# A transformer layer on one core: normalisation passes moved between engines, tile loads on another queue, and the last product in another order

## The chip, the core and the metric

The kernel runs on one core of a Trainium2 chip, in one launch. TensorE (PE) multiplies matrices into PSUM, VectorE (DVE) and ScalarE (ACT) work elementwise, GpSimd (POOL) works elementwise on SBUF, and SyncE (SP) issues DMAs. ScalarE issues some DMAs too. The metric is the device time of the launch in microseconds. Lower is better.

## The reference, cut to what matters

One post-norm layer over 2048 tokens of 1024 features: a mixer of two attentions and a short convolution, then a squared-ReLU MLP. Each half ends in a gated residual and a layer norm with a gain and a bias. The change touches what follows the mixer:

```python
def layer_norm(x, g, b):
    mu = x.mean(-1, keepdims=True)
    var = jnp.square(x - mu).mean(-1, keepdims=True)
    return ((x - mu) * lax.rsqrt(var + EPS)) * g + b
...
y_x = jnp.concatenate([mo, go, co], axis=-1) @ w_o                 # output projection
x = layer_norm(ALPHA * x + mx[:, 2] * y_x, ln1_g[l], ln1_b[l])
y_x = jnp.square(jax.nn.relu((x * (1.0 + mx[:, 4]) + mx[:, 3]) @ w1)) @ w2
x = layer_norm(ALPHA * x + mx[:, 5] * y_x, ln2_g[l], ln2_b[l])
```

## The kernel before, in words

Matmuls run on numbers split in two parts: a high part (ScalarE copies and rounds it) and a low part (VectorE subtracts the high part from the number). A product of two split numbers is three matmuls: high x high, high x low, low x high. Six stages follow each other. A stage begins when the one before has ended on all engines. Only the last two are touched.

**stage_mix, the output projection** (line 1259 on, about 1764 to 2006 us). It works over 16 tiles of 128 tokens, in the order of TILE. For tile s, TensorE (`work`, then `turn`) multiplies the mixed tile `m_hi`, `m_lo` (1 MB, loaded by `load_m`, two buffers) by w_o, 48 matmuls of 128x512, and then transposes the normalised rows of the tile before. VectorE (`work`) applies the gate, adds the residual, takes the statistics, waits for ScalarE's square root, centres and scales (`o_r`) and multiplies by the gain `ln_g` into `x1`. GpSimd adds the bias `ln_b` (line 1488). SP stores x1. ScalarE makes the modulated, transposed tile (`stream`), and then, per pair of tiles, the high parts of the seven operands for the MLP (`highs`, line 1397). Five of these are sums of two blocks, which GpSimd forms (`sums`, line 1482, two buffers). VectorE makes the low parts (`lows`, line 1467). Results that don't fit in SBUF go through a ring of three buffers to DRAM on SP's queue. VectorE's order is: tile 2q, the low parts of the pair before, tile 2q+1. ScalarE issues `load_x` and `load_m` for tile s+2 behind the square root of tile s.

**stage_mlp, the MLP** (line 1520 on). Both matrices are multiplied by Strassen's scheme: seven products of half-size blocks in place of eight, over sums of blocks. The first matrix (2009 to 2632 us) isn't touched. For the second, the 2048 tokens are two halves `hf`; per half there are seven products in the order of ORDER2, 14 in all (PRODS). A product is 8 chunks of 24 matmuls (128x512) over four row blocks `tt`, into four PSUM banks. For each chunk SP loads x (512 KB) and one or two blocks of w2 (512 KB each); where there are two, GpSimd forms their sum (`chunk_sum`, line 2090); ScalarE makes two high parts (`chunk_high`), VectorE two low parts (`chunk_low`, lines 1936 and 1938). Products 2 and 5 need no sum. The function `steps` lays down one order for all engines: at chunk tau they prepare chunk tau + 5 (AHEAD), then treat the product that ended before. In its chunks 0 and 1 they add its four banks into the result quarters `yacc` (`evacuate` on VectorE, line 2016, `first` on ScalarE for a quarter's first use); in 2 and 3 they apply gate and residual and take the statistics of quarters that are complete (`before_ln`, lines 2024 to 2029; PRES names them, x1 is read again from DRAM into two buffers); in 4 and 5 they finish complete tiles (FINISH, after products 6 and 7): ScalarE centres and scales (line 1904), VectorE multiplies by the gain (line 2055), GpSimd adds the bias (line 2118), SP stores. SP's queue holds these stores between the chunk loads. GpSimd's bias passes stand between its chunk sums.

The last product runs apart: for each row block tt in turn all 8 chunks, 48 matmuls. `last` treats each row block as it comes: add, gate, residual, statistics, norm and, one row block later, the gain.

## Time and profile before

| | us |
|---|---|
| median of 3 runs | 3297.54 (3292.43 to 3299.11) |
| the profiled execution | 3291.43 |
| its span, first to last instruction | 3289.6 |
| TensorE busy | 3093.5 |
| VectorE busy | 2354.3 |
| GpSimd busy | 1470.7 |
| ScalarE busy | 1365.4 |

All times in the rows are microseconds from the start of the span of one profiled execution. The time of a launch is the span and some 2 us around it. A matmul's duration in the rows is longer than its step to the next one, as they are pipelined: starts are to be compared. An idle time in brackets is that of the engine before the instruction, with what ended it.

### The profile page before, as it was taken

What the parts mean: (1) busy time and instruction counts of PE and PEld (TensorE: products, weight loads), DVE (VectorE), ACT (ScalarE), POOL (GpSimd) and SP (SyncE); (2) the same over time, 40 slices, a digit from 0 to 9 for tenths busy, and PEclk for the clock granted to TensorE, in tenths of its full rate; (3) what the DMA queues carried; (4) which work ended last, traced back from release to release, by engine and by line L of the source; (5) the groups of instructions that cost most, each with busy time, mean ns of one, the idle gap of its engine ahead of it and who ended that gap; (6) DMA issues with size and microseconds to landing.
All of it is one profiled execution on the core that took longest, in us unless ns stands there. A gap on an engine that the chain in (4) does not pass through costs nothing. (4 is left out here: it accounts for less than half of the span.)

```text
span 3289.6 us, 38729 instructions
## 1 busy us (share of the span) xinstructions
PE 3093.5 (94%) x13713; PEld 2283.2 (69%) x13713; DVE 2354.3 (72%) x3209; ACT 1365.4 (42%) x1931; POOL 1470.7 (45%) x857
## 2 busy tenths in 40 slices
PE   6999958999999999999998897999999999999996
PEld 3888845565565655656565775888788888887885
DVE  4344447777777777777765888777778768887778
ACT  3222222434344343444442435655555554344432
POOL 1233301576665766765662445333333223444453
PEclk8999977999999999999998998999999999999998
DMA  6222378123332223230214577444734488777873
GB/s 236 62 88 85 90 239 271 53 57 83 87 82 74 56 61 87 67 80 14 54 35 165 224 260 292 161 158 156 291 144 150 152 311 293 289 265 275 299 288 137
DMA packets 235708, 515.51 MB, mean 157 GB/s; under 512 B 26704, under 2 KB 101840, under 8 KB 223312
## 3 DMA queue, kind: packets, MB, share of 16 engines
q1 hardware_dynamic: 224688, 472.39, 43.0%
q10 hardware_dynamic: 10848, 40.90, 3.5%
q8 instruction: 99, 1.62, 0.2%
q14 instruction: 73, 0.60, 0.1%
HBM read 356.64 MB, written 156.57 MB: 156 GB/s over the span
## 5 line engine op out<-in xcount | busy, mean ns | idle before, releaser
L1032 DVE TENSOR_REDUCE h_mpart<-a_mx 128x1 f32<-128x512 f32 x920 | 568.3, 636 | 260.6 <-PE a_mx L1121 251.7
L978 POOL TENSOR_TENSOR a_acc_p<-a_acc_p,a_pf 128x1024 f32<-128x1024 f32 x240 | 582.0, 2425 | 234.2 <-ACT a_pf L1014 213.0
L1014 ACT ACTIVATE a_pf<-a_sc 128x1024 f32<-128x1024 f32 x432 | 443.0, 1026 | 475.5 <-PE a_sc L1147 470.2
L2148 PE MATMUL f_bank<-slot_hi,f_wx 128*128 128x512 f32 x1280 | 401.0, 390 | 9.0 <-DVE f_wx L1931 7.0
L2081 POOL TENSOR_TENSOR f_work<-raw_rows 128x512 f32<-128x512 f32 x160 | 220.9, 1382 | 369.8 <-DVE f_wx L1931 366.4
L2090 POOL TENSOR_TENSOR f_y<-f_y,raw_rows 128x1024 f32<-128x1024 f32 x80 | 222.0, 2776 | 333.2 <-DMA raw_rows<-in_w 333.2
L2148 PE MATMUL f_bank<-slot_lo,f_wx 128*128 128x512 f32 x896 | 350.0, 391 | 0.0
L2148 PEld LDWEIGHTS f_bank<-slot_hi,f_wx 128*128 128x128 f32 x1280 | 240.9, 188 | 60.4 <-DVE f_wx L1931 7.4
L2156 PE MATMUL f_bank<-slot_hi 128*128 128x512 f32 x672 | 263.9, 393 | 12.4 <-DVE slot_lo L1938 12.4
L1952 DVE TENSOR_TENSOR f_work<-f_work,f_bank 128x512 f32<-128x512 f32 x256 | 174.4, 681 | 134.3 <-ACT f_work L1821 123.1
L2156 PE MATMUL f_bank<-slot_lo,slot_hi 128*128 128x512 f32 x672 | 263.6, 392 | 0.0
L2156 PE MATMUL f_bank<-slot_hi,slot_lo 128*128 128x512 f32 x672 | 263.4, 392 | 0.0
L500 PE MATMUL p_main<-win_hi,u_hi 128*128 128x512 f32 (+2 forms) x528 | 198.2, 375 | 20.3 <-POOL u_lo L443 19.6
L1938 DVE TENSOR_TENSOR slot_lo<-f_y,slot_hi 128x1024 fp32r<-128x1024 f32 x84 | 138.6, 1650 | 94.1 <-ACT slot_hi L1805 93.5
L1121 PE MATMUL a_mx<-a_mk_hi,a_mq_hi 96*128 96x512 f32 (+1 forms) x480 | 186.7, 389 | 10.7 <-DVE h_mpart L1032 10.5
L500 PE MATMUL p_main<-win_lo,u_hi 128*128 128x512 f32 (+2 forms) x528 | 196.3, 372 | 0.0
L500 PE MATMUL p_main<-win_hi,u_lo 128*128 128x512 f32 (+2 forms) x528 | 196.1, 371 | 0.0
L2148 PEld LDWEIGHTS f_bank<-slot_lo,f_wx 128*128 128x128 f32 x896 | 169.2, 189 | 34.9
L1164 PE MATMUL a_o<-a_pf,h_gv 128*64 128x512 f32 x864 | 192.8, 595 | 0.0
L1164 PE MATMUL a_o<-a_pf,a_v 128*64 128x512 f32 x864 | 192.7, 595 | 0.0
L1147 PE MATMUL a_sc<-a_mq_hi,a_mk_hi 97*128 97x512 f32 x432 | 177.2, 410 | 0.0
L1147 PE MATMUL a_sc<-h_gq_hl,h_gk_hh 128*128 128x512 f32 x432 | 176.3, 408 | 0.7 <-ACT h_gq_hm L994 0.7
(288 smaller groups left out, 6545.1 us busy)
## 6 DMA issues: line engine op xcount, KB each, us to landing
raw_rows<-s_hx SPq DMA_DIRECT2D x112, 512.0 KB, 4.1
f_y<-in_w SPq DMA_DIRECT2D x112, 512.0 KB, 5.2
raw_rows<-in_w SPq DMA_DIRECT2D x80, 512.0 KB, 5.8
raw_rows<-in_w SPq DMA_DIRECT2D x32, 1024.0 KB, 4.8
s_hx<-stream SPq DMA_DIRECT2D x128, 256.0 KB, 2.7
s_hx<-f_work SPq DMA_DIRECT2D x96, 256.0 KB, 2.0
a_wa<-in_w_ada SPq DMA_DIRECT2D x8, 2048.0 KB, 9.0
s_mix<-low SPq DMA_DIRECT2D x96, 128.0 KB, 2.5
```

Of the source, the lines that this page charges most:

```text
L500: mm = nc.tensor.matmul(main[:, b, 0:cn], lhs[s][:, k], rhs[:, k, c0:c0 + cn], start=(k == 0 and rhs is w_hi and lhs is u_hi), stop=(k == ...
L978: nc.gpsimd.tensor_tensor(acc[:, :], left[:, :], pf[(b * KT + kt) % NPF][:, :], ALU.add).then_inc(added_p, 1)
L1014: nc.scalar.activation(pf[n % NPF][:, :], sc[n % 2][:, :], ACT.Exp, scale=SCALES[0 if is_mla(b) else 1]).then_inc(exped, 1)
L1032: nc.vector.reduce_max(mpart[b % 2][:, s, k:k + 1], mx[c % 2][:, 0:CHUNKS[k][1]], AX.X).then_inc(mx_read, 1)
L1121: nc.tensor.matmul(mx[c % 2][:, 0:width], lhs, rhs, start=True, stop=True).then_inc(mx_done, 1)
L1147: mm = nc.tensor.matmul(out, x, y, start=(m == 0), stop=(m == len(ops) - 1))
L1164: mm = nc.tensor.matmul(o_ps[half * DH:(half + 1) * DH, :], v[0 if is_mla(b) else 1][:, kt], pf[n % NPF][:, half * QB:(half + 1) * QB], st ...
L1952: nc.vector.tensor_tensor(t, t, bank[:, (NP * n + pos) % 8, :], plus(sign)).then_inc(c_set, 1)
L2081: nc.gpsimd.tensor_tensor(out, w1_part(n, first), w1_part(n, second), plus(sign)).then_inc(sum_set, 1)
L2090: nc.gpsimd.tensor_tensor(y1[cc % YN], y1[cc % YN], y2[k % Y2N], plus(sign)).then_inc(y_sum, 1)
L2148: mm = nc.tensor.matmul(by_pair(bank[:, m % 8, :]), w[:, k], x[s][:, :, k * P:(k + 1) * P], start=(k == 0 and j == 0), stop=(k == 3 and j ...
L2156: mm = nc.tensor.matmul(bank[:, 4 * (pr % 2) + tt, :], x[s][:, f, tok], y[s][:, 2 + f, :], start=(start and j == 0), stop=(stop and j == 2))
```

## The change

In the output projection the loads of the mixed tiles move from ScalarE's queue to SP's. `load_m(s + 2)` goes ahead of the ring stores and of the store of x1, and the ring stores come one tile later in the program. The bias moves from GpSimd to VectorE.

In the MLP the order of products becomes 2, 4, 3, 1, 6, 5, 7. PRES, DVE_ADDS and ACT_FIRST follow from it. ScalarE no longer centres, GpSimd no longer adds the bias: VectorE does (y - mean) * gain and then y * rstd + bias. ScalarE's first writes of the second half wait for the stored tiles of their own quarter only. The last product takes its first three chunks over all row blocks together. Gate and residual of the last quarter are applied before it, and its banks are scaled by the gate on their own and added.

```diff
         @block.sync
         def _(sp):
+            def load_m(s):
+                t = TILE[s]
+                if s >= 2:
+                    sp.wait_ge(y_done, s - 1)
+                for part, m in enumerate((m_hi, m_lo)):
+                    sp.dma_start(raw(m[s % 2]), g.mix[part][t]).then_inc(mix_in[s % 2], 16)
+            load_m(0)
             sp.dma_start(ln_cols[:, :], a["ln1_cols"]).then_inc(cols_in, 16)
...
             for s, t in enumerate(TILE):
+                if s + 2 < TT:
+                    load_m(s + 2)
+                if s and s % 2 == 0:
+                    store_sums(s // 2 - 1)
                 sp.wait_ge(x1_set, s + 1)
                 sp.dma_start(g.x1[t * P:(t + 1) * P, :], x1[s % 2]).then_inc(x1_stored[s % 2], 16)
-                p = s // 2
-                if s % 2 and p < PAIRS:
-                    for pos in range(NP):
-                        use = ring_use(p, pos)
-                        if use is None:
-                            continue
-                        sp.wait_ge(lo_set, NP * p + pos + 1)
-                        for part, at in enumerate((ring_hi, ring_lo)):
-                            sp.dma_start(g.uc[p // 4, pos, part][:, p % 4, :], raw(at[use % RING])).then_inc(uc_stored[use % RING], 32 // 2)
             sp.wait_ge(cols_in, 16)
...
         @block.scalar
-            def load_m(s):
-                t = TILE[s]
-                if s >= 2:
-                    act.wait_ge(y_done, s - 1)
-                for part, m in enumerate((m_hi, m_lo)):
-                    act.dma_start(raw(m[s % 2]), g.mix[part][t]).then_inc(mix_in[s % 2], 16)
...
                 nc.scalar.activation(rstd[:, :], var[:, :], ACT.Sqrt).then_inc(std_set, 1)
                 if s + 2 < TT:
                     load_x(s + 2)
-                    load_m(s + 2)
                 if s and (s - 1) % 2:
                     highs((s - 1) // 2)
...
                     dve.wait_ge(x1_stored[s % 2], 16 * (s // 2))
                 nc.vector.tensor_tensor(x1[s % 2], at, ln_g, ALU.mult).then_inc(scaled, 1)
+                dve.wait_ge(scaled, s + 1)
+                nc.vector.tensor_tensor(x1[s % 2], x1[s % 2], ln_b, ALU.add).then_inc(x1_set, 1)
                 assert seen[0] == STEPS, seen
...
-                pool.wait_ge(scaled, s + 1)
-                nc.gpsimd.tensor_tensor(x1[s % 2], x1[s % 2], ln_b, ALU.add).then_inc(x1_set, 1)
...
-        ORDER2 = (5, 3, 2, 4, 1, 6, 7)
+        ORDER2 = (2, 4, 3, 1, 6, 5, 7)
...
-        DVE_ADDS = {5: (), 3: (("12", 1),), 2: (("22", -1),), 4: (("11", 1), ("21", 1)), 1: (("11", 1), ("22", 1)), 6: (("22", 1),), 7: (("11", 1),)}
-        ACT_FIRST = {5: (("12", 1), ("11", -1)), 3: (("22", 1),), 2: (("21", 1),), 4: (), 1: (), 6: (), 7: ()}
+        DVE_ADDS = {2: (), 4: (("21", 1),), 3: (("22", 1),), 1: (("11", 1), ("22", 1)), 6: (("22", 1),), 5: (("12", 1), ("11", -1)), 7: (("11", 1),)}
+        ACT_FIRST = {2: (("21", 1), ("22", -1)), 4: (("11", 1),), 3: (("12", 1),), 1: (), 6: (), 5: (), 7: ()}
...
-        PRES = {3: ("12",), 4: ("21",), 6: ("22",), 7: ("11",)}
-        PRE_ORDER = ("12", "21", "22", "11")
+        PRES = {4: ("21",), 6: ("22",), 5: ("12",), 7: ("11",)}
+        PRE_ORDER = ("21", "22", "12", "11")
         FINISH = {6: range(4, 8), 7: range(0, 4)}
-
-        def steps(prep, evacuate, before_ln, finish, last):
+        TOGETHER = 3
+
+        def steps(prep, evacuate, before_ln, finish, last, before_last=lambda tt: None):
...
                     for key in PRES.get(i, ()):
                         for tt in (2 * k - 4, 2 * k - 3):
                             before_ln(hf, key, tt, pr)
-                elif k < 6 and i in FINISH:
-                    finish(hf, FINISH[i], k - 4)
+                elif k < 6:
+                    if i in FINISH:
+                        finish(hf, FINISH[i], k - 4)
+                    if pr == LAST - 1:
+                        for tt in (2 * k - 8, 2 * k - 7):
+                            before_last(tt)
             last()
...
 
             def store_out(hf, t):
-                k = finish_index(hf, t)
-                if k == 15:
-                    sp.wait_ge(last_set, 1)
-                else:
-                    sp.wait_ge(biased, k + 1)
-                sp.dma_start(a["out"][0, hf * 1024 + t * P:hf * 1024 + (t + 1) * P, :], yacc[t]).then_inc(out_stored, 16)
+                sp.wait_ge(scaled, finish_index(hf, t) + 1)
+                sp.dma_start(a["out"][0, hf * 1024 + t * P:hf * 1024 + (t + 1) * P, :], yacc[t]).then_inc(last_stored if hf else out_stored[t // 4], 16)
 
             for n in range(PAIRS):
...
-                        act.wait_ge(out_stored, 16 * 8)
+                        act.wait_ge(out_stored[int(key[0]) - 1], 16 * 4)
                     elif pr == 0:
...
-                nc.scalar.activation(yacc[t], yacc[t], ACT.Identity, scale=rstd[:, t:t + 1], bias=shift[:, t:t + 1]).then_inc(centred, 1)
-
             def before_ln(hf, key, tt, pr):
                 if key in ("22", "11") and tt == 3:
...
-                link(nc.vector.tensor_tensor(shift[:, c], mv[:, c, 0], rstd[:, c], ALU.mult))
-                nc.vector.tensor_scalar(shift[:, c], shift[:, c], -1.0, None, ALU.mult).then_inc(norm_ready, 1)
 
             def scale(hf, t):
                 k = finish_index(hf, t)
+                dve.wait_ge(rows_in, 32)
+                nc.vector.scalar_tensor_tensor(out=yacc[t], in0=yacc[t], scalar=mv[:, t, 0:1], in1=ln_g, op0=ALU.subtract, op1=ALU.mult).then_inc(centred, 1)
                 dve.wait_ge(centred, k + 1)
-                dve.wait_ge(rows_in, 32)
-                nc.vector.tensor_tensor(yacc[t], yacc[t], ln_g, ALU.mult).then_inc(scaled, 1)
+                nc.vector.scalar_tensor_tensor(out=yacc[t], in0=yacc[t], scalar=rstd[:, t:t + 1], in1=ln_b, op0=ALU.mult, op1=ALU.add).then_inc(scaled, 1)
...
+            def residual(hf, key, tt):
+                k = pre_index(hf, key, tt)
+                half = int(key[1]) - 1
+                y = quad(key, tt)
+                dve.wait_ge(gate_step, 2)
+                nc.vector.tensor_tensor(y, y, gate[:, half * 512:(half + 1) * 512], ALU.mult).then_inc(mid, 1)
+                dve.wait_ge(mid, k + 1)
+                dve.wait_ge(x1_in[k % X1N], 16 * (k // X1N + 1))
+                nc.vector.scalar_tensor_tensor(out=y, in0=x1[k % X1N], scalar=ALPHA, in1=y, op0=ALU.mult, op1=ALU.add).then_inc(pre_set, 1)
+                dve.wait_ge(pre_set, k + 1)
+
+            def before_last(tt):
+                dve.wait_ge(add_set, adds_before(LAST))
+                residual(1, "11", tt)
+
             def last():
                 for tt in range(4):
-                    evacuate(LAST, tt)
-                    before_ln(1, "11", tt, LAST)
-                    norms(1, tt, 1, pre_index(1, "11", tt))
-                    if tt:
-                        scale(1, tt - 1)
-                scale(1, 3)
-                dve.wait_ge(scaled, TT)
-                nc.vector.tensor_tensor(yacc[3], yacc[3], ln_b, ALU.add).then_inc(last_set, 1)
-            steps(chunk_low, evacuate, before_ln, finish, last)
+                    k, part = pre_index(1, "11", tt), y1[tt % YN][:, 0, :]
+                    y = quad("11", tt)
+                    dve.wait_ge(tt_done, 4 * LAST + tt + 1)
+                    nc.vector.tensor_tensor(part, bank[:, 4 * (LAST % 2) + tt, :], gate[:, 0:512], ALU.mult).then_inc(last_mid, 1)
+                    dve.wait_ge(last_mid, tt + 1)
+                    nc.vector.tensor_tensor(y, y, part, ALU.add).then_inc(add_set, 1)
+                    dve.wait_ge(add_set, adds_before(LAST) + tt + 1)
+                    nc.vector.bn_stats(stats[:, tt, 0, :], y).then_inc(stat_set, 1)
+                    norms(1, tt, 1, k)
+                    scale(1, tt)
+            steps(chunk_low, evacuate, before_ln, finish, last, before_last)
...
-            def bias(hf, t):
-                k = finish_index(hf, t)
-                pool.wait_ge(scaled, k + 1)
-                pool.wait_ge(rows_in, 32)
-                nc.gpsimd.tensor_tensor(yacc[t], yacc[t], ln_b, ALU.add).then_inc(biased, 1)
...
+            for c in range(TOGETHER):
+                cc = LAST * CH + c
+                pe.wait_ge(clo, 2 * cc + 2)
+                for f in range(2):
+                    for tt in range(4):
+                        if c == 0 and f == 0:
+                            pe.wait_ge(add_set, adds_before(LAST - 2) + len(DVE_ADDS[PRODS[LAST - 2][1]]) * (tt + 1))
+                        two(LAST, tt, chunk_slot(cc), f, c == 0 and f == 0, False)
             for tt in range(4):
-                pe.wait_ge(add_set, adds_before(LAST - 2) + len(DVE_ADDS[PRODS[LAST - 2][1]]) * (tt + 1))
-                for c in range(CH):
+                for c in range(TOGETHER, CH):
                     cc = LAST * CH + c
                     pe.wait_ge(clo, 2 * cc + 2)
                     for f in range(2):
-                        mm = two(LAST, tt, chunk_slot(cc), f, c == 0 and f == 0, c == CH - 1 and f == 1)
+                        mm = two(LAST, tt, chunk_slot(cc), f, False, c == CH - 1 and f == 1)
                 mm.then_inc(tt_done, 1)
```

## Rows read from the trace of the kernel before

**Rows 1.** The page: busy us of each engine, share of the span, instructions

```profile
PE 3093.5 (94%) x13713; PEld 2283.2 (69%) x13713; DVE 2354.3 (72%) x3209; ACT 1365.4 (42%) x1931; POOL 1470.7 (45%) x857
```

**Rows 2.** Windows: length; busy of PE, PEld, DVE, ACT, POOL; clock; DMA share; GB/s

```profile
1796.00:2002.00 206.00, 177.03 (x801) 144.58 (x799) 169.18 (x259) 75.79 (x185) 87.50 (x51) 0.94 0.62 232
2633.00:3211.00 578.00, 569.81 (x2500) 470.87 (x2499) 451.81 (x383) 247.08 (x261) 238.88 (x85) 0.99 0.80 289
...
3211.00:3290.00 79.00, 49.19 (x195) 38.69 (x193) 64.22 (x101) 17.74 (x20) 29.51 (x11) 0.80 0.34 128
```

**Rows 3.** Waits, 1760 to 2010 us: who waited for whom, us in total, times, longest

```profile
DVE o_ring_lo L1467 <- ACT o_ring_hi L1397: 18.4, 20, 2.9
...
PE o_y L1502 <- DMA slot_lo<-s_mix: 16.7, 7, 3.3
...
PE o_t_x L1511 <- DVE o_r L1451: 14.6, 5, 9.6
```

**Rows 4.** Timeline, VectorE and GpSimd, output projection: start, duration, line, tiles, [idle before]

```profile
1809.18 1.23 DVE L1437 SCALAR_TENSOR_TENSOR o_r<-o_x,o_r 128x1024 f32<-128x1024 f32 x1
...
1816.75 0.69 DVE L1467 TENSOR_TENSOR slot_lo<-o_total,slot_hi 128x512 fp32r<-128x512 f32 x1
...
1824.16 2.52 DVE L1467 TENSOR_TENSOR o_ring_lo<-o_total,o_ring_hi 128x512 fp32r<-128x512 f32 x1 [0.28 <-ACT o_ring_hi L1397]
...
1835.32 2.34 DVE L1437 SCALAR_TENSOR_TENSOR o_r<-o_x,o_r 128x1024 f32<-128x1024 f32 x1
...
1915.88 1.23 DVE L1436 TENSOR_TENSOR o_r<-o_y,o_gate 128x1024 f32<-128x1024 f32 x1 [1.79 <-PE o_y L1502]
...
1823.29 2.85 POOL L1488 TENSOR_TENSOR o_x<-o_x,o_ln_b 128x1024 f32<-128x1024 f32 x1
...
2001.03 2.34 POOL L1488 TENSOR_TENSOR o_x<-o_x,o_ln_b 128x1024 f32<-128x1024 f32 x1 [8.09 <-DVE o_x L1456]
```

**Rows 5.** Timeline, TensorE and ScalarE (ACTq is its DMA issues), 1891 to 1894 us

```profile
1891.24 0.73 PE L1502 MATMUL o_y<-low,slot_hi 128*128 128x512 f32 x2 [3.16 <-DMA slot_lo<-s_mix]
...
1893.86 0.49 ACTq L1363 DMA_DIRECT2D slot_hi<-s_mix  x1
```

**Rows 6.** Timeline, TensorE, second MLP matrix and its last product

```profile
2633.24 0.48 PE L2156 MATMUL f_bank<-slot_hi 128*128 128x512 f32 x1
...
3008.11 0.80 PE L2156 MATMUL f_bank<-slot_hi 128*128 128x512 f32 x1 [6.16 <-DVE slot_lo L1938]
...
3211.29 0.39 PE L2156 MATMUL f_bank<-slot_hi 128*128 128x512 f32 x1
...
3217.86 0.39 PE L2156 MATMUL f_bank<-slot_hi,slot_lo 128*128 128x512 f32 x1
...
3231.36 0.80 PE L2156 MATMUL f_bank<-low 128*128 128x512 f32 x1 [0.54 <-DVE slot_lo L1938]
...
3267.99 0.39 PE L2156 MATMUL f_bank<-low,slot_lo 128*128 128x512 f32 x1
```

**Rows 7.** Timeline, GpSimd, 2980 to 3010 us

```profile
2983.19 6.65 POOL L2118 TENSOR_TENSOR f_work<-f_work,f_ln_b 128x1024 f32<-128x1024 f32 x2 [10.97 <-DVE f_work L2055]
```

**Rows 8.** Timeline, VectorE, the last row blocks

```profile
3270.37 0.69 DVE L2029 BATCH_NORM_STATS2 cond_pad<-f_work 128x6 f32<-128x512 f32 x1
...
3272.54 0.16 DVE L2047 TENSOR_TENSOR cond_pad<-cond_pad 128x1 f32<-128x1 f32 x1
...
3274.15 0.68 DVE L2016 TENSOR_TENSOR f_work<-f_work,f_bank 128x512 f32<-128x512 f32 x1
...
3285.37 1.23 DVE L2070 TENSOR_TENSOR f_work<-f_work,f_ln_b 128x1024 f32<-128x1024 f32 x1
```

**Rows 9.** Timeline, VectorE, four residual quarters; and its costliest group, 2633 to 3290 us

```profile
3231.23 0.68 DVE L2024 TENSOR_TENSOR f_work<-f_work,f_gate 128x512 f32<-128x512 f32 x1
...
3238.81 0.69 DVE L2029 BATCH_NORM_STATS2 cond_pad<-stream 128x6 f32<-128x512 f32 x1
...
L1936 DVE TENSOR_TENSOR slot_lo<-raw_rows,slot_hi 128x1024 fp32r<-128x1024 f32 x83 | 145.9, 1758 | 19.3 <-ACT slot_hi L1799 18.8
```

47 lines of the change are left out of this document (20 added, 27 removed).

## The prediction

> **What bounds the kernel now.** I read the page first: its busy shares say that TensorE is near its limit over the whole span, so only stretches in which it waits can give time back [rows 1]. The windows say where these are: 1796 to 2002 us (the output projection, 177.0 us busy of 206), 2633 to 3211 us (the second MLP matrix up to its last product, where only about 8 us are idle) and 3211 to 3290 us (the last product and the end, 49.2 us busy of 79) [rows 2]. The attention and the first MLP matrix, which the change leaves alone, are not looked at.
>
> In the output projection the table of waits gives TensorE's pauses: 16.7 us for the loads of the mixed tiles and 14.6 us for VectorE's normalised rows. Of these 2.6 us lie at the start and 9.6 us at the end, so 19.0 us lie in the middle [rows 3]. Yet VectorE is what sets the pace there: it waited for TensorE's product twice only (1.8 us in the row shown, 1.9 us the other time) and ran 169 us of 206 [rows 2, 4]. The mixed tile comes late because ScalarE issues its load only after a square root that waits for VectorE: the load goes out at 1893.9 us, while TensorE had already been kept 3.2 us for the one before [rows 5]. So the load's lateness is mostly an image of VectorE's.
>
> In the last MLP part a matmul takes 0.2266 us (29 steps from 3211.29 to 3217.86 us), a product of 192 of them 43.5 us. Thirteen products from 2633.24 us would end at 3198.8 us; the last one begins at 3211.3, so 12.5 us were lost, mainly in and after the pause of 6.2 us that ends at 3008 us and a smaller one ahead of it, when GpSimd was adding the bias (6.65 us for two tiles) ahead of its block sums. The last product took from 3211.3 to 3268.2 us, 56.9 instead of 43.5 us: its first row block asks for all eight chunks within 11 us, and they aren't there [rows 6, 7]. From 3268.2 to the span's end at 3289.6 us another 21.4 us pass, as VectorE is behind: it takes up the last row block at 3274.15 us [rows 8].
>
> **The change part by part.** The sum is made against the profiled execution: 3291.4 us, with a span of 3289.6 us. It is 6.1 us under the median of the three runs, and I subtract the same gain from the median.
>
> *Output projection.* Bias on VectorE: a two-input pass over 128x1024 takes 1.23 us, and passes follow each other at 1.26 [rows 4]. Sixteen are added. For the first two tiles VectorE waits for TensorE anyway; the other fourteen add 14 x 1.25 = 17.5 us to its chain, which runs from 1807.9 to 2001.0 us. What it gets back: while GpSimd adds the bias, VectorE's two-input passes over SBUF stand still. The pass at 1824.16 us lasts 2.52 us where the same shape lasts 0.69 (GpSimd's bias runs from 1823.29), the one at 1835.32 lasts 2.34 us where 1.23 is usual. I count six of the first kind and four of the second: 6 x 1.83 + 4 x 1.11 = 15.4 us. The two waits for TensorE, 3.7 us, go too, since the tile loads no longer hang on ScalarE's square root. Chain: 17.5 - 15.4 - 3.7 = -1.6 us. The last bias takes 1.23 instead of 2.34 us, another -1.1 [rows 4]. Together -2.7 us. Bounds: no relief at all gives 17.5 - 3.7 - 1.1 = +12.7; if the 18.4 us in which VectorE waits for ScalarE's high parts [rows 3] hid all of the new passes, -19.
>
> Of the moved loads every issue counts: two issues of 0.49 us leave ScalarE's queue per tile [rows 5] and join SP's. There, a load now stands ahead of the ring stores and of the stored rows. For even tiles it waits for a product that is long done. For odd ones it stands behind the seven ring stores, so it goes out when VectorE has finished its low parts, some 4 us sooner than now. TensorE has slack against VectorE there, so it costs nothing; without that slack it would be a pause of about 1 us per pair, 7 us in all. ScalarE's weight copies begin 2 us sooner, but VectorE then waits for the columns: nothing.
>
> A page of the Trainium skill, DMA: Bandwidth & Descriptors, section Issuing engines are not separate DMA queues, says that another issuing engine saves only the time of issuing; by it alone the two waits would stay and this part would be +1.0 us. The pause behind the square root [rows 5] is a place in program order, which that rule doesn't cover, so I go by the row.
>
> *Second MLP matrix, before the last product.* Centring leaves ScalarE, the bias leaves GpSimd, VectorE has two passes (subtract the mean and scale; multiply and add the bias) instead of one. For 16 tiles that is 16 x 1.25 = 20 us more, less two tiny steps in each of the norms, less the passes that the bias held. GpSimd's block sums are never behind a bias again, and SP's store of a tile, with the chunk loads queued behind it, waits for VectorE alone. The new order parts the two heavy finishes (products 6 and 7) by product 5, which needs no sums and one load less per chunk. The load on VectorE in the block after product 6 or 7: 16 low-part passes of 1.21 us, 19.4; four adds, 2.7; four residual quarters at (3239.50 - 3231.23) / 4 = 2.07 us, 8.3; norms 2; two passes on each of four tiles, 9.9; and what block sums hold up. The mean low-part pass is 1.76 us against 1.21 free, so 0.55 x 16 = 9 us at most for a block [rows 9]. Together 51 us against 43.5. The five chunks that are prepared ahead are 27 us of matmuls, and the block before or after has 35 to 40 us of work: covered. If that cover is gone, 7.5 us are lost three times. I keep 3 of the 12.5 us of loss, so -9.5 us; bounds 0 and 22 kept.
>
> *Last product.* The first three chunks go over all four row blocks (16.3 us), then each row block takes its five others in 6.8 us. With P for the product's start, chunk 7 is needed at P + 21.8. In before it was ready 20.1 us after the start (TensorE took it up at 3231.36, the last pause, 0.5 us), behind a run of products with sums; now product 5 stands ahead. So no pause: 43.5 instead of 56.9 us, -13.4. Bounds: -13.4 and 0.
>
> *The end.* The gate and the residual of the last quarter are done ahead, in the shadow of the matmuls. VectorE in this product: eight adds 5.4, two chunks 4.8, four quarters 8.3, four residuals 5.6, thus free at about P + 24; the first row block is ready at P + 23.1. Then per row block: scale and add, a pass of 0.68 us each and the step to the next, 1.5 in all, statistics to the end of the norm 2.33 (3270.37 to 3272.70 us), two passes 2.5: 6.4 us, under the 6.8 of the matmuls. So after the last matmul come 0.3 + 6.4 us and the store, which takes 3.0 (3286.6 to 3289.6 us) [rows 8]: 9.7 instead of 21.4, -11.7 us. If VectorE lags by 8 us, that much comes on top.
>
> Sum: -2.7 - 9.5 - 13.4 - 11.7 = -37.3 us. Profiled 3254.1 us; from the median 3297.5, 3260 us.
>
> **The rivals.**
> *The bias costs VectorE in full in the output projection* (the sums take the place of the bias in holding it): +12.7 instead of -2.7, 3276 us. For it: VectorE is already the pace there. Against it: the held passes are in the rows. [...]
> *TensorE sets the pace there*: its 19.0 us of pauses go instead of 2.7, 3244 us. For it: VectorE's 18.4 us of waits could absorb the new passes. Against: those waits follow a chain of sum, high part, low part that the change leaves.
> *Stalls stay and VectorE is behind at the end*: +9.5 and +8, 3278 us. For it: 51 against 43.5 us of work in some blocks. Against: the lead.
> *The joined last product does nothing*, because chunks come at a pace that no order mends: +13.4, 3274 us.
> *Slower than before*: VectorE's 24 new-form passes before the last product are each held by a block sum (3.4 instead of 1.2 us, 53 us) and 12 more passes cost 15: 68 us, which nothing covers if the lead is empty whenever a finish begins; 3328 us. It decides from 37 us uncovered. Against it: the lead is refilled in every block between.
>
> **How the numbers follow.** Forecast 0.58; bias in full 0.10; TensorE's pace 0.10; stalls and lag 0.12; last product no better 0.06; slower 0.04. The likeliest gives 3260 us. The range 3244 to 3277 us takes in all but the slower case, about half of the stalls case and some of the edges, some 15 in 100. A change of 0.2%, 6.6 us, is about what a measurement of this kernel can tell from none. All cases but the last lie further below; faster 0.94, same 0.02, slower 0.04.
>
> **What would show it.** Right: in the output projection VectorE's low-part passes of 2.5 us are gone and its chain is about as long as before; GpSimd's only work is block sums; no pause over 3 us between 2633 us and the last product; the last product lasts 44 us; 9 to 11 us from the last matmul to the end. Wrong: TensorE waiting for the low parts in the blocks with a finish, two-input passes of 3.4 us among the new ones, VectorE taking up the last row block later than 1 us after its matmuls, or an output projection over 5 us longer.

## The result, and the profile after

The changed kernel takes 3275.5 us (median of 6 runs, 3267.5 to 3279.3) against 3299.2 us for the kernel before, timed beside it (6 runs, 3292.4 to 3303.3). The ratio is 0.9927, 95% interval 0.9915 to 0.9940: 24 us less, 20 to 28. The forecast was 3260 us with a range of 3244 to 3277; the sign and the range held, the range by 1.5 us, but 13 of the 37 us that the sum promised did not come. The two profiled executions lie closer together, 3275.5 and 3291.4 us: the profiled one of the kernel before is 7.8 us faster than its median, that of the changed kernel is at its median. So the profiles can show some 16 of the 24 us.

A line of the page, busy us of each engine, the changed kernel (before: [rows 1]):

```profile
PE 3082.6 (94%) x13713; PEld 2276.9 (70%) x13713; DVE 2358.5 (72%) x3230; ACT 1346.7 (41%) x1915; POOL 1382.3 (42%) x826
```

GpSimd lost 88 us and VectorE gained only 4, although it took over every bias: most of what it took over, it gets back in passes that are held less (17.1 us in the output projection alone, as worked out at the end). In windows of the three stretches (length; busy of PE, PEld, DVE, ACT, POOL; clock; DMA share; GB/s), answering [rows 2]:

```profile
1773.00:1999.00 226.00, 196.19 (x896) 160.01 (x896) 186.07 (x298) 84.74 (x200) 53.15 (x37) 0.95 0.67 245
2625.00:3197.00 572.00, 568.32 (x2503) 469.87 (x2503) 457.54 (x395) 237.85 (x253) 207.44 (x76) 1.00 0.80 290
3197.00:3273.00 76.00, 48.31 (x196) 38.04 (x194) 64.24 (x95) 10.12 (x13) 12.31 (x5) 0.81 0.40 146
```

The last row is the finding of the case. TensorE was to be busy in 44 of the 53 us behind the start of the last product; it is busy in 48 of 76, as it was in 49 of 79 before, and VectorE works 64 of the 76 us.

**Output projection.** Waits, 1755 to 2005 us (who waited for whom, us in total, times, longest), answering [rows 3]:

```profile
PE o_t_x L1513 <- DVE o_r L1453: 18.9, 6, 13.3
DVE o_ring_lo L1471 <- ACT o_ring_hi L1400: 16.5, 20, 2.0
DVE o_u_cols L1415 <- DMA o_ln_cols<-in_ln_cols: 13.2, 1, 13.2
...
PE o_y L1504 <- DVE slot_lo L1421: 7.0, 2, 6.6
...
PE o_y L1504 <- DMA slot_lo<-s_mix: 5.5, 6, 1.5
DVE o_r L1438 <- PE o_y L1504: 3.7, 2, 3.0
```

TensorE's waits for the mixed tiles fell from 16.7 to 5.5 us. Its waits for VectorE's normalised rows rose from 14.6 to 18.9 us: VectorE sets the pace of the stage, now as before. A new wait stands at the start: VectorE waits 13.2 us for the columns, and TensorE 6.6 us for the low part behind them. Timeline of VectorE, and one block sum of GpSimd, answering [rows 4]:

```profile
1822.04 1.28 DVE L1471 TENSOR_TENSOR o_ring_lo<-o_total,o_ring_hi 128x512 fp32r<-128x512 f32 x2
...
1834.74 1.22 DVE L1460 TENSOR_TENSOR o_x<-o_x,o_ln_b 128x1024 f32<-128x1024 f32 x1
...
1837.14 1.23 DVE L1439 SCALAR_TENSOR_TENSOR o_r<-o_x,o_r 128x1024 f32<-128x1024 f32 x1
...
1822.86 2.86 POOL L1486 TENSOR_TENSOR o_total<-stream 128x512 f32<-128x512 f32 x2 [1.29 <-DVE o_ring_lo L1471]
```

The passes that took 2.52 and 2.34 us in [rows 4] take 0.64 and 1.23. The bias (L1460) costs 1.22, as it was priced.

**Last MLP part.** TensorE's timeline, answering [rows 6]; the second, fourth, fifth and sixth rows are all its pauses over 1 us:

```profile
2625.75 0.48 PE L2151 MATMUL f_bank<-slot_hi 128*128 128x512 f32 x1
...
2993.64 0.50 PE L2151 MATMUL f_bank<-slot_hi 128*128 128x512 f32 x1 [3.13 <-DVE slot_lo L1935]
...
3197.54 0.39 PE L2151 MATMUL f_bank<-slot_hi 128*128 128x512 f32 x1
...
3218.99 0.50 PE L2151 MATMUL f_bank<-slot_hi 128*128 128x512 f32 x1 [2.25 <-DVE slot_lo L1935]
...
3225.81 0.80 PE L2151 MATMUL f_bank<-low 128*128 128x512 f32 x1 [4.70 <-DVE slot_lo L1935]
...
3230.47 0.80 PE L2151 MATMUL f_bank<-low 128*128 128x512 f32 x1 [1.73 <-DVE slot_lo L1935]
...
3253.60 0.39 PE L2151 MATMUL f_bank<-low,slot_lo 128*128 128x512 f32 x1
```

The last product begins at P = 3197.5 us and ends 56.4 us later; its three pauses are 8.7 us together, and some 4 more go in the matmuls behind them: from 3216 to 3235 us the granted clock averages 0.64, between full speed (2.4 GHz) and the lower level (1.2 GHz), and a matmul right behind a pause shows 0.80 us instead of 0.39. VectorE over the same time, answering [rows 8] (its waits in brackets), and SP's last store:

```profile
3144.84 1.22 DVE L1935 TENSOR_TENSOR slot_lo<-f_y,slot_hi 128x1024 fp32r<-128x1024 f32 x1
...
3162.97 1.28 DVE L2013 TENSOR_TENSOR f_work<-f_work,f_bank 128x512 f32<-128x512 f32 x2
...
3196.07 3.42 DVE L1935 TENSOR_TENSOR slot_lo<-f_y,slot_hi 128x1024 fp32r<-128x1024 f32 x1
...
3203.24 3.31 DVE L2046 SCALAR_TENSOR_TENSOR stream<-stream,cond_pad,f_ln_b 128x1024 f32<-128x1024 f32 x1
...
3217.71 1.23 DVE L1935 TENSOR_TENSOR slot_lo<-f_y,slot_hi 128x1024 fp32r<-128x1024 f32 x1 [3.79 <-ACT slot_hi L1811]
...
3245.14 0.69 DVE L2072 TENSOR_TENSOR f_y<-f_bank,f_gate 128x512 f32<-128x512 f32 x1
...
3251.49 0.68 DVE L2072 TENSOR_TENSOR f_y<-f_bank,f_gate 128x512 f32<-128x512 f32 x1
...
3269.28 1.28 DVE L2046 SCALAR_TENSOR_TENSOR f_work<-f_work,cond_pad,f_ln_b 128x1024 f32<-128x1024 f32 x1
...
3270.60 0.33 SPq L1727 DMA_DIRECT2D out<-f_work  x1
```

The first row is the low part of chunk 96, ready at 3146.1 us; TensorE needs it at 3154.0, one product before P. VectorE should begin to add up the product finished at 3154.0, and does so at 3163.0. It takes up the first row block of the last product at 3245.1, P + 47.6 (I had said P + 24), and from there needs 6.34 us per row block (I had said 6.4).

### The profile page after: what moved, and what is told of

Its sections match the earlier page's. It is cut to its first block and busy times, and to the rows that moved or that the text cites. A ratio compares the mean times of both kernels' runs of the same rounds, so it can differ in the third digit from the quotient of the medians.

```text
span 3273.7 us, 38674 instructions
## 1 busy us (share of the span) xinstructions
PE 3082.6 (94%) x13713; PEld 2276.9 (70%) x13713; DVE 2358.5 (72%) x3230; ACT 1346.7 (41%) x1915; POOL 1382.3 (42%) x826
## 5 line engine op out<-in xcount | busy, mean ns | idle before, releaser
L500 PE MATMUL p_main<-win_hi,u_hi 128*128 128x512 f32 (+2 forms) x528 | 197.5, 374 | 19.7 <-POOL u_lo L443 19.0
L1935 DVE TENSOR_TENSOR slot_lo<-f_y,slot_hi 128x1024 fp32r<-128x1024 f32 x84 | 127.4, 1517 | 83.1 <-ACT slot_hi L1811 82.3
```

The lines of the kernel that those rows point to most:

```text
L500: mm = nc.tensor.matmul(main[:, b, 0:cn], lhs[s][:, k], rhs[:, k, c0:c0 + cn], start=(k == 0 and rhs is w_hi and lhs is u_hi), stop=(k == ...
L1935: nc.vector.tensor_tensor(slot_lo[s][:, 2:4, :], y1[cc % YN], slot_hi[s][:, 2:4, :], ALU.subtract).then_inc(clo, 1)
```

## The experiments

The theories. **D**: in the last 110 us VectorE's queue sets the end; TensorE's pauses there are a symptom. **T**, my forecast's: TensorE's last product sets it. Beside them **A**, the normalisation of tiles 4 to 7 ahead of the last product fills VectorE; **B**, SP's stores of these tiles block the chunk loads; **C**, the chunks arrive too slowly in the four products with sums before, so the lead is gone. For the output projection **L** (the loads) and **Bias** (the held passes).

Stretches of all profiles, one execution each, in us. "Output projection" is from the first matmul on the gate row (L1216) to the first matmul of the MLP; "second matrix" from its first matmul to P; then P to the last matmul; the last matmul to the end of the span; P to the span's end; and P to VectorE's first pass on the last product's first row block ("take-up", which only kernels with the early residual have).

| kernel | output proj. | second matrix | P to last matmul | then to the end | P to the end | take-up |
|---|---|---|---|---|---|---|
| before | 244.5 | 578.1 | 57.1 | 21.2 | 78.3 | |
| changed | 236.6 | 571.8 | 56.4 | 19.7 | 76.1 | P + 47.6 |
| mix_only | 237.5 | 577.5 | 57.6 | 22.6 | 80.2 | |
| mlp_only | 245.5 | 572.8 | 54.5 | 19.3 | 73.8 | P + 45.3 |
| mix_loads | 242.8 | 578.5 | 63.6 | 21.1 | 84.7 | |
| mix_bias | 243.2 | 577.2 | 60.8 | 22.7 | 83.5 | |
| cols_first | 236.2 | 573.3 | 57.7 | 21.2 | 78.9 | P + 50.3 |
| late_stores | 237.2 | 565.9 | 55.0 | 19.9 | 74.9 | P + 46.4 |
| joined_none | 237.8 | 574.2 | 65.6 | 9.6 | 75.2 | P + 44.3 |
| old_order | 238.4 | 574.3 | 44.0 | 36.1 | 80.1 | P + 51.6 |
| no_finish | 238.1 | 570.2 | 50.6 | 19.7 | 70.3 | P + 41.7 |
| thin_11 | 237.3 | 570.2 | 43.7 | 19.7 | 63.4 | P + 34.8 |
| spread | 237.9 | 569.6 | 60.4 | 19.3 | 79.7 | P + 51.2 |
| best | 235.8 | 571.0 | 59.5 | 19.6 | 79.1 | P + 50.6 |

Two things are read off before any single row. The first MLP matrix, which no kernel here changes, takes 624.5 to 626.6 us in all of them. And where the output projection begins moves between 1754.9 and 1768.0 us although everything ahead of it is the same code: a comparison of whole spans from one profile each can be 10 us off. A comparison by stretches leaves that out, but each stretch is still one execution. Where the code of a stretch is the same, the output projection agrees within 2 us (236.6 to 238.4 in eight kernels), the second matrix only within 8 us (565.9 to 574.2 in changed, mlp_only, cols_first, late_stores and joined_none; 577.2 to 578.5 in the four with the old MLP), and P to the end within 5 to 6 us (73.8 to 78.9 in the three with exactly the new MLP, 78.3 to 84.7 with the old one). So a difference of a few us behind the start of the second matrix proves nothing by itself.

**mix_only and mlp_only: the two halves apart.** The kernel before with one stage of the changed kernel each:

```diff
mix_only:  - stage_mix of before        mlp_only:  - stage_mlp of before
           + stage_mix of the change               + stage_mlp of the change
```

> The kernel before with the changed output projection alone (bias on VectorE, low parts in one piece of two columns, loads moved); the second MLP matrix and the end stay as before. If the two halves of the change are independent, as my forecast took for granted, this gives what the stage shows in the profile after: MLP's first product 9.2 us sooner, so 8 to 10 us under the kernel before (ratio 0.997). My forecast's own term was 2.7 us. If the faster stage only moved a wait into the MLP (its first weight sums and high parts not ready when VectorE comes sooner), under 4 us remain of it.

> The kernel before with the changed MLP stage alone (new order of the products, additions moved, last product's first three chunks joined, residual of the last quarter ahead). Forecast by its terms: 9.5 + 13.4 + 11.7 = 34.6 us less. By the profile of the changed kernel: 23.7 in all less 9.2 in the output projection leaves 14 to 16 us (ratio 0.9953). If the late last product comes from the output projection's new timing or its DMAs, this one comes out better than that, by 20 us or more.

Measured: mix_only 0.9967 (0.9948 to 0.9986), 11 us less; mlp_only 0.9963 (0.9947 to 0.9980), 12 us less. Together 23, the changed kernel 24: the halves add up, as far as these intervals can tell. The late last product does not come from the output projection either: with the old one, in mlp_only, it takes 54.5 us. By stretches mix_only gains 7.0 us in the output projection and nothing in the MLP; mlp_only gains 9.8 from the second matrix's start to the end, and nothing in the output projection. So the stretches of these two account for 17 us, and those of the changed kernel's own profile for 16. The rest of the 24 us is about what the profiled execution of the kernel before lies under its median, and can't be placed in any stretch.

**mix_loads and mix_bias: the output projection apart.** mix_loads is mix_only with the bias back on GpSimd; mix_bias is the kernel before with the bias on VectorE and nothing else. (The low parts "in one piece" and "as in the change" of two expectations name no edit: the stages differ in the loads, the ring stores and the bias alone.)

```diff
 mix_loads (stage_mix of the change)
-                dve.wait_ge(scaled, s + 1)
-                nc.vector.tensor_tensor(x1[s % 2], x1[s % 2], ln_b, ALU.add).then_inc(x1_set, 1)
+                pool.wait_ge(scaled, s + 1)
+                nc.gpsimd.tensor_tensor(x1[s % 2], x1[s % 2], ln_b, ALU.add).then_inc(x1_set, 1)
 mix_bias (stage_mix of before): the same four lines with the signs turned
```

> The kernel before with the changed output projection's loads and the order of its queues alone: the loads of the odd tiles and ring stores moved, low parts and block sums as in the change, but the normalisation bias stays with GpSimd; the MLP as before. Theory L (the 7.3 us that the output projection gained beyond my 2.7 come from the loads that now arrive in time: TensorE's waits for DMA fell from 14.1 to about 6 us): this kernel alone brings 5 us or more in the stage, MLP's first product starts 4 to 8 us sooner than before. Theory B (they come from VectorE's passes no longer held by GpSimd's bias): MLP's first product starts within 3 us of the kernel before, and passes of 2.5 us stay in VectorE's rows.

> The kernel before with one edit: the normalisation bias of the output projection goes from GpSimd to VectorE. My forecast's terms for this edit: 15 passes of 1.25 us more on VectorE less 15.4 us of passes that GpSimd held, less the last bias, in all -2.7 us. Theory B: 5 us or more of the stage's 9.2 us come from it. Theory L: within 3 us of the kernel before. Low parts of 2.5 us beside the bias should be gone from VectorE's rows either way.

Measured: mix_loads 0.9984 (0.9967 to 1.0001), mix_bias 0.9982 (0.9967 to 0.9996), 5 to 6 us less each, hardly to be told from no change. By stretches 1.7 and 1.3 us, and both together 7 to 8. So neither theory: each edit alone uncovers what the other one mends. VectorE's 31 low parts by shape (busy, mean ns, idle before) and TensorE's waits for loads, first mix_loads, then mix_bias:

```profile
L1469 DVE TENSOR_TENSOR o_ring_lo<-o_total,o_ring_hi 128x512 fp32r<-128x512 f32 x31 | 40.0, 1300 | 17.3 <-ACT o_ring_hi L1400 17.3
...
PE o_y L1504 <- DMA slot_lo<-s_mix: 1.5, 5, 0.4
```

```profile
L1469 DVE TENSOR_TENSOR o_ring_lo<-o_total,o_ring_hi 128x512 fp32r<-128x512 f32 x31 | 27.2, 888 | 17.4 <-ACT o_ring_hi L1397 17.4
...
PE o_y L1502 <- DMA slot_lo<-s_mix: 14.8, 5, 3.5
...
DVE o_r L1436 <- PE o_y L1502: 8.1, 4, 3.0
```

With the loads alone TensorE is supplied (1.5 us of waits), but VectorE's low parts are still held (1300 ns). With the bias alone the low parts are free (888 ns), but the loads are late (14.8 us) and VectorE now waits for TensorE (8.1 us). Between the first matmul and the MLP, 238.1 us before: the loads bring 5.6, the bias 1.2, both 10.8 (227.3 in mix_only). Against it stands a loss of 3.8 us ahead of the first matmul, in every kernel whose loads are moved as in the change (10.1 us from the gate row to it instead of 6.4).

**cols_first: the loss at the start.**

```diff
-            load_m(0)
             sp.dma_start(ln_cols[:, :], a["ln1_cols"]).then_inc(cols_in, 16)
+            load_m(0)
```

> The changed kernel with one line moved: the load of the normalisation's columns is issued ahead of the first weight load of the output projection instead of behind it. Theory: in the changed kernel that load lands 4.6 us later than before and TensorE's first matmul of the stage waits for it, so this gives back 2 to 4 us (ratio to before 0.9918 or so) and VectorE's wait for the columns at the stage's start falls from 13.2 to about 9 us. Rival: the weight load lands later by as much and its low part becomes the last wait, nothing is gained (0.9927).

(What stands behind the columns now is the load of the first mixed tile, which the expectation calls a weight load.) Measured: 0.9918 (0.9901 to 0.9934) against 0.9927. In the profile VectorE's wait for the columns falls by 6.3 us, but TensorE's start comes only 1.9 us sooner (8.2 us behind the gate row):

```profile
DVE o_u_cols L1415 <- DMA o_ln_cols<-in_ln_cols: 6.9, 1, 6.9
```

```profile
1766.07 1.22 PE L1504 MATMUL o_y<-low,slot_hi 128*128 128x512 f32 x2 [4.42 <-DVE slot_lo L1421]
1766.07 0.50 PEld L1504 LDWEIGHTS o_y<-low,slot_hi 128*128 128x128 f32 x2 [4.71 <-DMA slot_lo<-s_mix]
```

The first row names VectorE's low part, but the first of these was ready at 1762.6 us. TensorE's weight load, in the second row, waits for what came last: the second half of the first mixed tile. It lands 8.1 us behind the gate row; in the kernel before it landed 6.3 us behind it, and TensorE started then. What differs is ScalarE's queue, first here, then before:

```profile
1757.87 0.85 ACTq L1374 DMA_DIRECT2D o_x<-in_x  x2
```

```profile
1765.07 0.45 ACTq L1369 DMA_DIRECT2D o_x<-in_x  x1
```

Before, ScalarE issued both halves of the first mixed tile and only then the first tile of x. Now it has no mixed tiles to issue and sends out both tiles of x at once, beside SP's loads. The second mixed tile is no cause: it is issued 1.3 us behind the gate row, as before. So the columns' place in SP's queue costs 2 us, and for the other 2 the traces offer the tiles of x that go out beside the first mixed tile; no run puts them back. The 2 us are under what the timing can tell.

**joined_none: does the last product set the end?**

```diff
-            for c in range(TOGETHER):        (three chunks over all four row blocks)
-            ...
-            for tt in range(4):
-                for c in range(TOGETHER, CH):
+            for tt in range(4):
+                pe.wait_ge(add_set, adds_before(LAST - 2) + ...)
+                for c in range(CH):
```

> The changed kernel with the last product not joined: each row block takes all its eight chunks before the next begins. Theory D (VectorE sets the end: from the evacuation of the product before the last but one at 3163 us it works almost without a gap to the end, so TensorE's pauses in the last product are a symptom): nothing changes, ratio to before 0.9927 within 0.0015, and VectorE still takes up its first last row block some 49 us after the last product starts. Theory of my forecast (TensorE's last product sets the end, its pauses cost): without the joined chunks TensorE waits for the last chunks' low parts in the first row block and does three row blocks behind them, 8 us or more are added (0.995).

Measured: 3275.3 us, ratio 0.9945 (0.9925 to 0.9965). The median is that of the changed kernel, but the kernel before was timed beside each of them and was faster here (3295.8 against 3299.2 us), so the ratio lies 0.0018 above the changed kernel's: outside the 0.0015 that D allowed, and at T's 0.995. The interval holds both, so the timing decides nothing. The profile does. TensorE's last matmul ends 65.6 us behind P, 9 later, and yet the end comes 75.2 us behind P (changed kernel: 76.1):

```profile
3206.69 0.79 PE L2151 MATMUL f_bank<-slot_hi 128*128 128x512 f32 x1 [6.92 <-DVE slot_lo L1935]
...
3260.70 0.39 PE L2151 MATMUL f_bank<-low,slot_lo 128*128 128x512 f32 x1
...
3261.12 0.69 DVE L2072 TENSOR_TENSOR f_y<-f_bank,f_gate 128x512 f32<-128x512 f32 x1 [2.19 <-PE f_bank L2151]
```

VectorE waits for TensorE once, for 2.2 us, at the last row block. With VectorE as late as it is, joining the chunks can be worth about those 2.2 us at most, where T has 9. T falls, by the profile.

**old_order: the order of the products back.** The joined last product and the early residual stay:

```diff
-        ORDER2 = (2, 4, 3, 1, 6, 5, 7)
+        ORDER2 = (5, 3, 2, 4, 1, 6, 7)
```

with the tables of additions that belong to it.

> The changed kernel with the order of the seven products of the second MLP matrix, and the split of their additions between VectorE and ScalarE, put back; the joined last product, the early residual of the last quarter and the changed output projection stay. Theory of my forecast: the order gives 9.5 us of its own and sets the start of the last product; without it, TensorE's stalls of 12.5 us return. By the VectorE-bound end the block with the normalisation of tiles 4 to 7 moves back to under the last product: VectorE reaches the last row blocks no sooner, and the time is 8 to 14 us above the changed kernel (ratio to before 0.996 to 0.998). Rival (the gain came from the residual ahead and from the joined chunks, the order only moves the late work): within 3 us of the changed kernel (0.993).

Measured: 3281.4 us, 0.9938 (0.9914 to 0.9961). That is inside the interval of the changed kernel, so the timing doesn't separate the two, and it is nearer to the rival's 0.993 than to the forecast's 0.996 to 0.998. The stretches give 6.5 us more (2.5 in the second matrix, 4.0 behind P), both within what executions of the same code differ by. The profile shows something better than a time:

```profile
3201.18 0.39 PE L2151 MATMUL f_bank<-slot_hi 128*128 128x512 f32 x1
...
3221.84 1.23 DVE L1935 TENSOR_TENSOR slot_lo<-f_y,low 128x1024 fp32r<-128x1024 f32 x1
...
3244.78 0.39 PE L2151 MATMUL f_bank<-low,slot_lo 128*128 128x512 f32 x1
...
3252.74 0.69 DVE L2072 TENSOR_TENSOR f_y<-f_bank,f_gate 128x512 f32<-128x512 f32 x1
```

Here the last chunk is ready at P + 21.9, the last product runs without a pause in 44.0 us, just as forecast, and the kernel still ends 80 us behind P, because VectorE normalises tiles 4 to 7 under that product instead of ahead of it and takes up the last row blocks at P + 51.6. TensorE finishing the last product in 44, 56 or 66 us gave ends at 80, 76 and 75 us: the end does not follow TensorE. That is D.

**late_stores: SP's stores out of the way.**

```diff
-                if k in (5, 6) and i in FINISH:
+                if k in (5, 6) and i in FINISH and pr != LAST - 2:
...
-            for t in FINISH[7]:
+            for t in (*FINISH[6], *FINISH[7]):
```

> The changed kernel with the stores of tiles 4 to 7 of the second half moved on SP's queue from among the last product's chunk loads to the end of the program. Theory B (SP waits for the scaled tiles, and the loads of chunks 108 to 111 stand behind that wait): the three pauses of TensorE in the last product (2.25, 4.70, 1.73 us) go, the last low part is ready some 8 us sooner, the time falls by 6 to 12 us (ratio 0.990 or less). Theory A (VectorE is full: 40.3 of 43 us busy with additions, normalisation and four scaled tiles in that block): the waits for DMA go, but the pauses stay within 2 us in sum and the time within 2 us.

Measured: 0.9934 (0.9917 to 0.9951). TensorE's waits for low parts behind 3150 us:

```profile
PE f_bank L2151 <- DVE slot_lo L1935: 7.5, 3, 5.2
```

7.5 us against 8.7, and no gain in time (3278.0 us): B falls.

**no_finish: VectorE's work taken away.** Its expectation says what is left out.

```diff
+                if hf and t >= 4:
+                    nc.vector.tensor_copy(tiny[:, t:t + 1], mv[:, t, 0:1]).then_inc(centred, 1)
+                    dve.wait_ge(centred, k + 1)
+                    nc.vector.tensor_copy(tiny[:, t:t + 1], mv[:, t, 0:1]).then_inc(scaled, 1)
+                    return
```

> The changed kernel with the normalisation's two passes over tiles 4 to 7 of the second half left out (these tiles are stored without it; 8 passes of 1.28 us, 10.3 us of VectorE's work in the block ahead of the last product). Theory D (VectorE's queue sets the end): the time falls by 8 to 12 us (ratio 0.990) and VectorE reaches the first last row block some 10 us sooner. Supply theory (the chunks' loads come late whatever VectorE does): the low parts of the last chunks come at the same time, VectorE idles instead, and the time falls by less than 4 us.

Measured: 3268.2 us, 0.9913 (0.9891 to 0.9936), an interval that still holds the changed kernel's 0.9927. P to the end is 70.3 us instead of 76.1, and under all three profiles with exactly the new MLP (73.8 to 78.9). Of 10.3 us of work removed some 6 come out, between the two expectations. Where the rest went is in VectorE's timeline:

```profile
3197.33 1.23 DVE L1935 TENSOR_TENSOR slot_lo<-f_y,slot_hi 128x1024 fp32r<-128x1024 f32 x1 [4.90 <-ACT slot_hi L1811]
3204.20 1.23 DVE L1935 TENSOR_TENSOR slot_lo<-f_y,slot_hi 128x1024 fp32r<-128x1024 f32 x1 [4.32 <-ACT slot_hi L1811]
3211.66 1.23 DVE L1935 TENSOR_TENSOR slot_lo<-f_y,slot_hi 128x1024 fp32r<-128x1024 f32 x1 [4.97 <-ACT slot_hi L1811]
```

14.2 us of waits for high parts (changed kernel, over the same stretch: 4.4), which in their turn wait for GpSimd's sums and these for their loads: the last product's chunks come every 7 us (low parts ready at 3190.4, 3198.6, 3205.4, 3212.9 and 3219.7 us). So A holds for about half of the work that was taken away; behind VectorE's work stands the supply.

**thin_11: the lead restored.** Also a kernel with less in it, as its expectation says.

```diff
+        right_of = lambda pr: ("11", None, 0) if pr == len(PRODS) - 3 else RIGHT[PRODS[pr][1]]
-        chunk_sums = [cc for cc in range(NCH) if RIGHT[PRODS[cc // CH][1]][1]]
+        chunk_sums = [cc for cc in range(NCH) if right_of(cc // CH)[1]]
```

and `right_of` at the three places where the chunks are loaded, summed and copied.

> The changed kernel with the second half's product 6 (the fourth of four products in a row whose weights are a sum of two blocks) computed from one block alone: its eight loads of 0.5 MB and GpSimd's eight sums are left out. Theory C (the chunks arrive at 5.4 us each there, 290 GB/s, so VectorE reaches that product's evacuation 10 us late and the lead is two chunks, not five): the evacuation begins within 3 us of the product's end, the first last row block comes 6 to 10 us sooner, and the time falls by 6 to 10 us (ratio 0.9905). Rival (the lead is spent in the block with the normalisation whatever comes before): under 3 us.

Measured: 3260.7 us, 0.9900 (0.9883 to 0.9916), 11 to 15 us under spread and joined_none, which were timed beside it and have the whole work (3271.7 and 3275.3); P to the end 63.4 us, 12.7 less. More than C expected:

```profile
3120.23 1.21 DVE L1936 TENSOR_TENSOR slot_lo<-f_y,slot_hi 128x1024 fp32r<-128x1024 f32 x1
...
3142.50 1.36 DVE L2014 TENSOR_TENSOR f_work<-f_work,f_bank 128x512 f32<-128x512 f32 x2 [4.65 <-PE f_bank L2152]
...
3187.86 0.39 PE L2152 MATMUL f_bank<-slot_hi 128*128 128x512 f32 x1
...
3222.69 0.69 DVE L2073 TENSOR_TENSOR f_y<-f_bank,f_gate 128x512 f32<-128x512 f32 x1
```

Chunk 96 is ready at 3121.4 us, 23 us ahead of its need at 3144.4 (changed kernel: 8.0 us). VectorE waits for the product to end instead of coming 9 us late, and takes up the last row blocks at P + 34.8. TensorE's last product runs in 43.7 us with no pause over 0.3 us. Chunks 89 to 93, made of one block here, come every 3.0 to 3.7 us; made of two in the changed kernel they come every 4.6 to 6.9. C holds, and it is the larger share. (The shares of A and C are not to be added: both free the same queue.) The edit takes away GpSimd's sums along with the loads, but the sums are not the pace: in the changed kernel GpSimd is busy 17.0 of the 43.5 us of that product and waits for the second block before every sum. Nor has VectorE less to do in that product (busy 32.4 us in the changed kernel, 33.0 here). By these rows it is the loads; whether their rate or the buffers that they wait for was not taken apart.

The new order has a part in this. When the last product but one begins, its first chunk, 96, had been ready for 17.5 us in the kernel before and for 14.0 in old_order, where a product with one block stands third in each half; the new order has four products with sums in a row there, and 8.0 us are left.

**spread: the same work, later.**

```diff
-                    if i in FINISH:
+                    if i in FINISH and pr != LAST - 2:
...
+                if tau - LAST * CH in (-2, -1, 0, 1):
+                    finish(1, (6 + tau - LAST * CH,), 0)
```

> The changed kernel with the same eight passes done later: one tile behind each of the low parts of chunks 107, 108, 109 and 110 instead of two behind 105 and two behind 106, and the stores of these tiles at the end. The chunk buffers come free sooner, so the loads run under the passes. Theory D with its idle time (1.3, 3.8 and 1.3 us for high parts and block sums in the last product): TensorE's pauses in the last product go or halve, VectorE's idle time goes, and the time falls by 3 to 6 us (ratio 0.991). Rival (VectorE's idle time comes from the pace of the loads alone): within 2 us of the changed kernel.

Measured: 3271.7 us, 0.9933 (0.9914 to 0.9952): no gain. The take-up is at P + 51.2. TensorE waits longer, in two pauses:

```profile
PE f_bank L2153 <- DVE slot_lo L1937: 12.5, 2, 8.3
```

The low parts of chunks 106 to 109 come sooner, those of 110 and 111 (P + 28.8 and P + 36) not; VectorE still has its 5 us of waits, and all of its work. The order within a full queue is worth nothing.

**best: the two mends together**, cols_first's lines and spread's:

> The changed kernel with both mends together: the columns' load first in the output projection, and the eight passes over tiles 4 to 7 spread behind the low parts of chunks 107 to 110 with their stores at the end. If the two add, 2 to 3 us from the first and about 2 us from the second: 4 to 5 us under the changed kernel, ratio to before 0.991. If VectorE sets the end, the second brings under 2 us, since no work of VectorE is removed: ratio 0.9918.

Measured: 3277.7 us, 0.9927 (0.9911 to 0.9944), the changed kernel's ratio exactly. No version that does the whole work was found that beats the changed kernel measurably.

## Why the prediction was right or wrong

**Output projection, -2.7 forecast, -7 to -8 found (stretch), -11 timed (-5 to -17).** The mechanism was right and the sizes too small on the gain's side. By shape, the low parts of [rows 4]'s kind went from 39.7 to 27.1 us and the residual's pass from 24.1 to 19.6: 17.1 us of relief where I counted 15.4. The bias is 19.6 us on VectorE, 16 passes of 1.22 as priced. VectorE's waits for TensorE fell by 6.1 us (9.8 to 3.7) where I had 3.7, its waits for high parts by 1.9, and its wait for ScalarE's first weight copies of the MLP by 2.5 (6.5 to 4.0), which I had priced at nothing. The two waits for TensorE that I had named (1.9 and 1.8 us) are gone; the other 2.4 us went at the first tiles. One price was missing, +3.8 us at the start: the columns' new place, of which cols_first gave back 1.9, and the tiles of x that ScalarE now issues beside the first mixed tile. My list of moved issues named the queues but looked only at the middle of the stage. And mix_loads and mix_bias show that the terms of this sum don't add one by one: 1.7 and 1.3 alone, 7 together.

The rival that the bias costs VectorE in full is out: mix_bias is no slower than before. The Trainium skill, Perfetto Trace Analysis, section Optimizing Scalar/DVE Operations, says that offloading a saturated VectorE may make sense, with the reservation that work shared between it and GpSimd might gain nothing; the trace agrees with the reservation, 2.52 us for a low part under a bias against 0.69 alone [rows 4].

**Second matrix, -9.5 forecast, -6.3 found** (571.8 against 578.1 us; the nine kernels with the new order lie between 565.9 and 574.2, mean 571.0, the four with the old MLP between 577.2 and 578.5). I kept 3 us of loss; about 6 are left, 3.1 of them in the pause at 2993.6 us. By old_order the order of the products has 2.5 us of the gain, which is within what executions of the same code differ by; that the rest is GpSimd's and ScalarE's relief is argued, not shown. The block with the finish of tiles 4 to 7 (2880.9 to 2894.2 us) made no pause over 1 us, as said. The one with the finish of tiles 0 to 3 (from 2974.7 us) did: its last pass, held by a block sum, and the two low parts behind it are what TensorE waits for at 2993.6 us.

```profile
2988.02 3.30 DVE L2046 SCALAR_TENSOR_TENSOR f_work<-f_work,cond_pad,f_ln_b 128x1024 f32<-128x1024 f32 x1
```

I had laid the pauses at this place in the kernel before (2.0 and 6.2 us) to GpSimd's bias. They do not hang on it alone: old_order, which has no bias on GpSimd, still pauses 5.7 us at 2998.0 us.

**Last product, -13.4 forecast, -0.7 found.** The step that failed is "So no pause", which rested on chunk 7 being ready at P + 20.1 because product 5 stands ahead. It was ready at P + 33. The joined loops do what was said of them when the chunks are there: 44.0 us in old_order, 43.7 in thin_11.

**The end, -11.7 forecast, -1.5 found.** The step that failed is "thus free at about P + 24". Its parts were right: eight adds, two chunks, four quarters, four residuals, and 6.34 us per row block. What was wrong is the point from which they were counted. VectorE was P + 47.6, and the difference of 23.5 us has three parts. First, 7.5 us: in the block before I counted 51 us of work against 43.5 and called the excess covered by the five chunks ahead. A lead covers TensorE, which is not kept waiting; it doesn't take the work away from VectorE, which carries it past P. Second, 9.0 us: VectorE began that block at 3163.0 instead of 3154.0, since the lead was 8.0 us and not 27, and its queue has the low parts up to five chunks ahead before the additions. The kernel before could have told me: there the lead at this point is 17.5 us, and VectorE begins the additions 11.0 us late. Third, 6.3 us of waits, 3.8 and 1.6 for high parts and 0.9 for the residual's rows. Together 24.1 + 7.5 + 9.0 + 6.3 = P + 46.9. (Measured, VectorE's work from there to the additions of the next product runs from 3163.0 to 3218.9 us: 55.9 us with 5.4 of the waits in it, so 50.5 of work, where I had 51.) The same sum for thin_11, where the block begins 1.9 us before the product ends and the waits are 6.2 us, gives P + 35.9; measured P + 34.8.

With VectorE at P + 47.6, the last two terms are no longer TensorE's: four row blocks of 6.34 and 3.1 us for the store give P + 76.1, which is the measured end, whatever the last product does (joined_none, old_order). So the -13.4 and the -11.7 were one term, VectorE's queue, and it moved by 2.2 us in the profile of the changed kernel, and by 5.4 between the means (81.7 us from P to the end in the four kernels with the old MLP, 76.3 in the three with exactly the new one; the two groups just overlap).

My own list named the sign: "VectorE taking up the last row block later than 1 us after its matmuls". It took it up at 3264.15, 10.2 us after them. Two more of its signs of being wrong came: TensorE waited for low parts in a block with a finish, and new-form passes took 3.3 us beside a block sum. Of the signs of being right the last product of 44 us, the 9 to 11 us behind it and, by 0.1 us, "no pause over 3 us" failed. Of the rivals "stalls stay and VectorE is behind at the end" comes nearest in kind, but not in place: half of the 12.5 us of stalls in the second matrix went, and the lag cost 23 us (12.7 in the last product, 10.2 behind it), not 8. "The joined last product does nothing" is right as to its effect and wrong as to its cause: TensorE's product does get shorter, in old_order, and nothing comes of it. That the median still fell inside the range is in part luck: 4 to 5 us of it come from the output projection, which gained more than I said, and the rest from the width that I gave for single cases.

**Open.** Why the last product's chunks come only every 7 us even when VectorE is not late (no_finish) was not tried. The profile offers the loads' waits for the buffers that the low parts free, and the loads of the residual's rows that stand in the same queue; neither was taken away alone. For buffers of another kind, those that the block sums free, there is this in no_finish, a block sum and the load of a second block behind it:

```profile
3200.68 2.40 POOL L2103 TENSOR_TENSOR f_y<-f_y,raw_rows 128x1024 f32<-128x1024 f32 x1 [4.48 <-DMA raw_rows<-in_w]
...
3203.10 0.33 SPq L1714 DMA_DIRECT2D raw_rows<-in_w  x1
```

Second blocks have two buffers, and this load goes out as the sum ends that frees one of them; so do the loads before and behind it (3196.23 and 3210.56 us). That fits too few buffers as the cause; a kernel with a third one was not tried.

## What to carry to other kernels

When one engine prepares another's work ahead, keep two books: the lead says whether the consumer waits, but the producer's own queue must be summed to the end of the program, from the last moment at which it was itself waiting, with nothing "covered". Read the lead from the trace (when a piece was ready against when it was needed), not from the program's depth: five chunks in the code were one and a half (8.0 us at 5.4 us each) at the place that mattered, and a little over three there in the kernel before. Before the consumer's last stretch is made shorter, look whether the producer is done by then; here it was not, and 12 us saved on TensorE in old_order bought nothing.
